# One decoder step on one core: attention with queries ahead, then eight steps of a head pair and a decode sequence; two tiles at a time where a feed-forward product begins

## The reference

```python
def mixer_mla(h, pos0, past_ckv, past_kpe, P):
    cq = rmsnorm(h @ P['mla_w_dq'], P['mla_g_q'])
    q = (cq @ P['mla_w_uq']).reshape(bsz, L, MLA_HEADS, MLA_NOPE + MLA_ROPE)      # 16 heads, 128 + 64
    q_nope, q_pe = q[..., :MLA_NOPE], rope(q[..., MLA_NOPE:], pos)
    kv = h @ P['mla_w_dkv']
    ckv = rmsnorm(kv[..., :MLA_KV_RANK], P['mla_g_kv'])                           # 256 wide
    kpe = rope(kv[:, :, None, MLA_KV_RANK:], pos)[:, :, 0]
    q_lat = jnp.einsum('blhd,rhd->blhr', q_nope, P['mla_w_uk'])
    o_lat = mla_attention(q_lat, q_pe, ckv, kpe, past_ckv, past_kpe)
    o = jnp.einsum('blhr,rhv->blhv', o_lat, P['mla_w_uv']).reshape(bsz, L, MLA_HEADS * MLA_V)
    return o @ P['mla_w_o'], ckv, kpe
```

## Time and profile before

| what | value |
|---|---|
| median of 3 runs | 3286.43 us (3283.92 to 3287.48) |
| the profiled execution, device time | 3291.61 us |
| its span, first to last instruction | 3289.7 us |
| granted TensorE clock, mean | 0.929 of full |
| TensorE busy | 90% of the span |
| VectorE / ScalarE busy | 42% / 40% |
| DMA, mean over the span | 105 GB/s |
| attention, head pairs | from 2216.7 to 2582.6 us |
| attention, decode sequences | from 2582.6 to 2743.5 us |

### The profile page before, as it was taken

The page is one execution under the profiler, slowest core; times in us unless marked ns, Lnnn a source line. Parts: engine busy times, 40 slices in busy tenths (PEclk is TensorE's granted clock), DMA queues, the critical chain, the costliest instruction groups (busy, mean ns, idle before and its releaser), DMA issues.

```text
span 3289.7 us, 56116 instructions
## 1 busy us (share of the span) xinstructions
PE 2976.2 (90%) x22503; PEld 2489.5 (76%) x22503; DVE 1379.9 (42%) x2522; ACT 1322.8 (40%) x1774; POOL 75.1 (2%) x139
## 2 busy tenths in 40 slices
PE   5999978999899989899998999989899678989996
PEld 3998858888688767799877998765665356779996
DVE  2444247788454553544335443312232213254433
ACT  3554345445222244554335553322222103365543
POOL 0000000000000000000000000000000120000000
PEclk7999988999889889999999999998999767999998
DMA  6223531222112223223432234411100474412221
GB/s 222 90 91 123 188 115 65 78 69 74 67 68 72 87 111 141 77 95 121 165 118 77 92 123 165 150 66 39 36 21 19 160 261 184 162 67 100 91 104 61
DMA packets 52952, 346.67 MB, mean 105 GB/s; under 512 B 7346, under 2 KB 7683, under 8 KB 23171
## 3 DMA queue, kind: packets, MB, share of 16 engines
q1 hardware_dynamic: 41906, 299.78, 25.4%
q0 software_dynamic: 10960, 45.71, 3.9%
HBM read 333.01 MB, written 12.45 MB: 105 GB/s over the span
## 4 chain that ended last, share of the span: by engine, by line
PE 81%; DVE 8%; ACT 4%; DVEq 2%; issue 2%; DMA 1%; ACTq 0%; SPq 0%; POOL 0%; PEldq 0%
PE PS L778 50%; PE PS L747 9%; PE PS L792 2%; PE PS L936 2%; PE PS L1132 2%; PE PS L1133 2%; PE PS L1145 1%; PE PS L1112 1%; PE PS L1187 1%; PE PS L1120 1%; PE PS L901 1%; PE PS L1162 1%; PE PS L761 1%; PE PS L800 1%; DMA weight_ring<-in_ada_w 1%
## 5 line engine op out<-in xcount | busy, mean ns | idle before, releaser
L1605 DVE TENSOR_TENSOR w_rest<-weight_ring,w_hi 128x1024 bf16<-128x1024 f32 (+1 forms) x304 | 363.7, 1197 | 960.5 <-ACT w_hi L1291 960.3
L1290 ACT ACTIVATE w_bf<-weight_ring 128x1024 bf16<-128x1024 f32 (+1 forms) x304 | 314.7, 1035 | 866.5 <-PE PS L778 859.3
L778 PE MATMUL PS<-hid_hi,w_hi 128*128 128x260 f32 x2752 | 371.6, 287 | 0.0
L778 PEld LDWEIGHTS PS<-hid_hi,w_hi 128*128 128x128 f32 x2752 | 340.1, 188 | 2.5
L778 PE MATMUL PS<-hid_rest,w_bf 128*128 128x260 bf16 x2752 | 337.6, 274 | 0.0
L778 PE MATMUL PS<-hid_bf,w_rest 128*128 128x260 bf16 x2752 | 335.6, 274 | 0.0
L1291 ACT ACTIVATE w_hi<-weight_ring 128x1024 fp32r<-128x1024 f32 (+1 forms) x304 | 309.9, 1019 | 0.0
L778 PEld LDWEIGHTS PS<-hid_bf,w_rest 128*128 128x128 bf16 x2752 | 266.6, 97 | 41.3
L778 PEld LDWEIGHTS PS<-hid_rest,w_bf 128*128 128x128 bf16 x2752 | 253.1, 97 | 44.3
L747 PE MATMUL PS<-hidden,weight_ring 128*128 128x260 f32 x896 | 206.3, 393 | 12.9 <-ACTq L504 8.9
L747 PEld LDWEIGHTS PS<-hidden,weight_ring 128*128 128x128 f32 x896 | 175.5, 197 | 42.3 <-ACTq L504 9.3
(11 more groups left out here) (386 smaller groups left out, 4168.6 us busy)
## 6 DMA issues: line engine op xcount, KB each, us to landing
weight_ring<-in_ffn_gu SPq DMA_DIRECT2D x88, 1024.0 KB, 4.8
ada_chunks<-in_ada_w SPq DMA_DIRECT2D x40, 1536.0 KB, 6.4
weight_ring<-in_ffn_wd SPq DMA_DIRECT2D x32, 1408.0 KB, 5.9
weight_ring<-in_w_hgrn SPq DMA_DIRECT2D x16, 1024.0 KB, 4.8
weight_ring<-in_ada_w SPq DMA_DIRECT2D x8, 1536.0 KB, 7.1
weight_ring<-in_w_ssm SPq DMA_DIRECT2D x8, 1536.0 KB, 6.4
weight_ring<-in_mla_pairs SPq DMA_DIRECT2D x8, 1536.0 KB, 6.4
arena<-in_pages SPq DMA_DIRECT2D x36, 288.0 KB, 5.9
```

What stands on the lines that cost most here:

```text
L778: last = pe.matmul(PS[:, bank + hf, 0:HT], w[:, buf, k * P:(k + 1) * P], x[:, first + k, hf * HT:(hf + 1) * HT], start=start and w is w_hi ...
L1290: act.activation(bf[:, buf, 0:n], src, ACT.Copy)
L1605: tt(WL_[:, buf, 0:n], W[:, slot, j * DC * P:j * DC * P + n], WH[:, buf, 0:n].bitcast(F32), ALU.subtract).then_inc(w_rest_ready, 1)
```

## The change

1. `head_pair` is split. A loop `queries` goes over all eight pairs first: query products, rotation, decode queries. The queries stay in SBUF (the 128-wide parts in `OC`, the rotary parts in `QPE`, which is `H`). Rotation's input is copied second of three.
2. The weights of a pair are loaded again for the second part, only the 8 tiles for keys and values (512 KB), under load numbers `LOADS["heads"]`.
3. Eight steps follow, written out one after the other on TensorE. Step n holds both heads of pair n and decode sequence n, interleaved by hand; the keys and values of pair n+1 are made in four pieces in between, through one PSUM bank (4). Score blocks go from the largest to the smallest, all 128-wide parts first. A head's probabilities and their transposes share one buffer for both heads.
4. In a decode sequence the exponentials use each partition's own maximum; the maximum over all partitions only gives a factor (`DST[:, 9:10]`) later on.
5. Pages lie in other buffers (parts of `Y`, `W`, the modulation chunks, the weight parts); SyncE issues all 16 of a sequence, GpSimd none. VectorE, not ScalarE, frees them.
6. `cut_group` makes w_hi first and w_bf second, each with its own semaphore; TensorE waits for w_bf before the second pass, and VectorE waits for it before it frees the slot.
7. `ffn_up` starts with `first_step`: for every normed chunk, one tile of both products.

The core of the diff:

```diff
@@ SyncE
-                    with sp.Fori(0, NB // 2) as b:
-                        for bb in range(2):
-                            sp.wait_ge(k_free[bb], b + 1)
-                            for pg in range(0, NPAGE, 2):
...
+                    base = LOADS["heads"]
+                    sp.wait_ge(w_free, base + 2)
+                    def head_weights(i, jj):
+                        slot = (base + jj) % 2
+                        sp.wait_ge(w_free, i * 2 + (base + jj + 1))
+                        sp.dma_start(WF[:, slot * HEAD_W:(slot + 1) * HEAD_W],
+                                     A["mla_pairs"][i * 2 + jj][:, 12 * P:20 * P]).then_inc(w_arrived[slot], 16)
+                    def pages_of(i, jj):
+                        sp.wait_ge(k_free[jj], i + 1)
+                        for pg in range(NPAGE):
...
+                    head_weights(0, 0)
+                    head_weights(0, 1)
+                    with sp.Fori(0, NB // 2 - 1) as i:
+                        for jj in range(2):
+                            pages_of(i, jj)
+                            head_weights(i, jj + 2)
+                    for jj in range(2):
+                        pages_of(NB // 2 - 1, jj)
+                    sp.wait_ge(k_free[0], NB // 2 + 1)
+                    sp.wait_ge(w_free, LOADS["uv"] + 2)
                     load(LOADS["uv"], 0, 0, 16, A["mla_uv"][0])
                     load(LOADS["uv"], 0, 1, 16, A["mla_uv"][1])
+                    sp.wait_ge(k_free[1], NB // 2 + 1)
@@ TensorE, start of an FFN
+                def first_step():
+                    g, buf = group(("up", s), 0, 0, 0)
+                    pe.wait_ge(gu_taken, f * FC + 1)
+                    for j in range(2):
+                        pe.wait_ge(w_bf_ready, g + j + 1)
+                        pe.wait_ge(w_rest_ready, g + j + 1)
+                    for k in range(DC):
+                        normed(k)
+                        for j in range(2):
+                            last = one_tile(2 * j, (buf + j) % 2, k, k, HH, HB, HL, k == 0, k == DC - 1)
+                            if k == DC - 1:
+                                last.then_inc(part_done, 1)
@@ TensorE, attention
+                def step(n, more):
+                    scores(n, 0)
+                    page_scores(n // 2, n % 2)
+                    transposes(n, 0)
+                    if more:
+                        key_piece(n + 1, 0)
+                    pe.wait_ge(b_m, n + 1)
+                    pe.matmul(PS[0:1, 7, 264:264 + P], DST[:, 2:3], IDENT, start=True, stop=True).then_inc(b_mt, 1)
+                    mixed(n, 0)
+                    pe.wait_ge(b_row, n + 1)
...
+                    pe.wait_ge(b_ex, n + 1)
+                    for j in range(4):
+                        pe.transpose(PS[:, 5, j * P:(j + 1) * P], PD[:, j, :], IDENT)
+                    pe.transpose(PS[0:NB, 6, 0:QR_], PDO, IDENT[0:QR_, 0:QR_]).then_inc(b_pt, 1)
+                    scores(n, 1)
+                    if more:
+                        value_piece(n + 1, 0)
+                    page_mix(n // 2, n % 2)
+                    transposes(n, 1)
+                    if more:
+                        key_piece(n + 1, 1)
+                    pe.wait_ge(b_sum, n + 1)
...
+                    mixed(n, 1)
+                    if more:
+                        value_piece(n + 1, 1)
+                    pe.wait_ge(b_on, n + 1)
...
@@ ScalarE, cut
-                act.activation(bf[:, buf, 0:n], src, ACT.Copy)
                 act.activation(hi[:, buf, 0:n], src, ACT.Copy).then_inc(w_hi_ready, 1)
+                act.activation(bf[:, buf, 0:n], src, ACT.Copy).then_inc(w_bf_ready, 1)
@@ VectorE, softmax of a head
+                def softmax(n, hh):
+                    row_max(n, hh, 3)
+                    for qb in (2, 1, 0):
+                        row_max(n, hh, qb)
+                        normalise(n, hh, qb + 1)
+                    normalise(n, hh, 0)
...
+                def step(i, jj, more):
+                    n = i * 2 + jj
+                    softmax(n, 0)
+                    own_max(n)
+                    common_max(n)
+                    softmax(n, 1)
+                    combine(n, jj)
+                    if more:
+                        queries(n + 1)
```

More of the change, by code:

```diff
@@ L1108, in head_pair, with key_piece @@
                     last.then_inc(p_ql, 1)
-                    uv = W[:, slot, 16 * P:20 * P].rearrange("p (a b) -> p a b", a=2)
-                    for c in range(NCH):
+                def key_piece(n, hh):
+                    if hh == 0:
+                        w_ready(pe, LOADS["heads"], 0, n)
+                    pe.wait_ge(p_kvc, 4 * n + 2 * hh)
+                    for k in range(RC):
+                        first = (LOADS["heads"] + n) % 2 * HEAD_W + (hh * 2 + k) * P
+                        last = pe.matmul(PS[:, 4, :], WF[:, first:first + P], CKV[:, k, 0:NP_],
+                                         start=(k == 0), stop=(k == RC - 1))
+                    last.then_inc(p_kv, 1)
@@ L1111, in head_pair, with value_piece @@
+                def value_piece(n, half):
+                    slot = (LOADS["heads"] + n) % 2
+                    uv = WF[:, slot * HEAD_W + 4 * P:(slot + 1) * HEAD_W].rearrange("p (a b) -> p a b", a=2)
+                    pe.wait_ge(p_kvc, 4 * n + 2 * half + 1)
+                    for c in (2 * half, 2 * half + 1):
                         for k in range(RC):
-                            last = pe.matmul(PS[:, 6 + c // 2, (c % 2) * 256:(c % 2 + 1) * 256],
+                            last = pe.matmul(PS[:, 4, (c % 2) * 256:(c % 2 + 1) * 256],
@@ L1199, in mla @@
                     for jj in range(2):
[L1200 removed]
+                        queries(i, jj)
                 fence()
@@ L1203, in mla @@
                     pe.sem_inc(k_free[bb], 1)
-                with pe.Fori(0, NB // 2) as b2:
-                    for bb in range(2):
-                        decode(b2, bb)
+                for half in range(2):
+                    key_piece(0, half)
+                    value_piece(0, half)
+                for n in range(NB):
+                    step(n, n + 1 < NB)
                 fence()
@@ L1519, in mla @@
+                for half in range(2):
+                    key_piece(0, 0, half)
+                    value_piece(0, 0, half)
+                with act.Fori(0, MH // 4 - 1) as i:
+                    for jj in range(2):
+                        step(i, jj, True)
+                for jj in range(2):
+                    step(MH // 4 - 1, jj, jj == 0)
                 fence()
@@ new lines, in step @@
+                def step(i, jj, more):
+                    n = i * 2 + jj
+                    softmax(n, 0)
[3 more added lines that the diff above has]
+                    combine(n, jj)
+                    if more:
+                        queries(n + 1)
+                queries(0)
+                with dve.Fori(0, MH // 4 - 1) as i:
+                    for jj in range(2):
+                        step(i, jj, True)
+                for jj in range(2):
+                    step(MH // 4 - 1, jj, jj == 0)
```

412 lines of the change are left out of this document (218 added, 194 removed).

## The result

The changed kernel takes 3146.4 us (median of 4 runs, 3144.9 to 3149.2) where the kernel before takes 3285.2 (3276.0 to 3287.5) beside it: a ratio of 0.958, with a 95% interval of 0.956 to 0.960, or 139 us less. Forecast were 3179 and a gain of 107.

A forecast was written before the change was run, and what follows sets the result against it. TensorE, busy 90% of the span, was taken as the bound, with time to gain in attention's waits and low clock. Gains of 85 + 3 + 13 + 2 + 4 = 107 us gave 3179 us from 3286.4, range 3145 to 3225.

The forecast's parts named there:

- the step: Attention, one head pair with one decode sequence: 40 us each, bounds 37.5 and 45, eight steps.
- the rival with the clock up: Attention and HGRN2: steps of 37.5 us, `mla_w_uv` at full clock, HGRN2 at its best; 3152 us, chance 0.17.
- `mla_w_uv`: Products right after attention: may run at full clock behind a dense step, 0 to 6 us less, taken as 3.
- a sign of being wrong: Inside a step: TensorE waiting for VectorE more than 3 us in total, or pages landing after their step's scores.
- the sign of being right: Chain of waits in attention: steps of 38 to 43 us, with a clock above 0.9.
- Queries and gap: Start of attention: queries of all pairs take 102 us, to 2319; first page scores at 2348, after a wait for pages.
- Waits for the softmax: Inside a step: TensorE waits 0 to 1.7 us at head 0 and 0 to 0.6 at head 1.
- the rival with lower clock: Steps: two pauses each leave half clock for 6 to 7 us, steps of 45 us; 3219 us, chance 0.17.
- FFN starts: Two tiles per normed chunk: 3.3 us less at each of four starts, 13 us in all, bounds 4 and 20.
- w_hi first: Weight copies: 2 us less at HGRN2's start and the output projections, 4 us less over eight HGRN2 heads.
- Pages and SyncE: Page loading by SyncE alone: issues 1.1 to 1.3 us apart, 22 us of slack per step hides added waits.
- The slower case: Steps: pauses and narrow page products keep the mean clock at 0.6, steps of 62 us; 3355 us, chance 0.04.

The follow-up runs named there:

- the kernel with decode apart: Changed kernel with eight steps of pairs alone, then eight of decode sequences alone, same instructions otherwise: 3303.1 us, 1.005 of the kernel before.
- both kernels with scores in separate order: Kernel before with a head's 128-wide scores ahead of its 64-wide ones: 3285.4 us; the same with weight transposes as fp32 products with the identity: 3299.1 us.
- plain products: Kernel before with the transposes of attention weights as fp32 matmuls with the identity: 3330.8 us, 1.014.
- The variant with complete blocks: Changed kernel with each score block's 128-wide and 64-wide parts one after the other, largest block first: 3137.5 us, and 3136.3 us in a second measurement.
- the two single edits: Changed kernel with one tile per normed chunk at FFN starts: 3163.0 us; changed kernel with w_bf written before w_hi: 3158.6 us.
- a second issuer: Changed kernel with odd pages issued by GpSimd: 3146.8 us, 0.957 of the kernel before.

## Why the prediction came out as it did

The sign, the order of the parts and the main mechanism (a sequence's work under a pair's) were right; the kernel with decode apart shows that the gain hangs on it. The size was not: the gain in attention was put 42 us too low (127 for 85), nearly all of that in one term, the step. The rest was 18 us for 22. The sum over the two profiled executions is 145 us; the medians are 139 apart.

That 3146 still lies in the range is luck. The range reached down to 3145 to take in the rival with the clock up, 3152; that rival wanted steps of 37.5 us, `mla_w_uv` at full clock and HGRN2 at its best. The steps are 34.0 to 36.0, all below that bound, and `mla_w_uv` did not come. What the prediction named as a sign of being wrong also came true: TensorE waits for VectorE inside a step by more than 3 us, 26.0 over eight steps and 3.2 or more in seven of them. And steps of 38 to 43 us, the sign of being right, did not come. The step was shorter than any bound because its work was overpriced, not because its waits were understood.

**Queries and gap: right.** From 2201.95 to the end of the eighth pair's queries, 2303.5, it is 101.6 us for 102; one pair takes 12.58. The first page scores started 128.2 us after the first query product, forecast 131.3, with a wait of 1.7 us for a page. The gap's parts were partly others than named: TensorE waits first for the weights of pair 0, which the prediction gives no time,

```profile
PE PS L1167 <- DMA weight_ring<-in_mla_pairs: 5.8, 1, 5.8
```

and for the pages much less than the 9 us that lie between 2319 + 20 and 2348.

**The step: 40 forecast, 34.65 measured** (277.2 us for eight). At full clock the terms were put at 35.6 us of work and 2.8 of waits, and 1.6 for clock; the fourth step has 30.87, 3.17 and none. (The waits that the prediction names, 1.7 and 0.6, make 2.3; for the other 0.5 in its 38.4 it gives no source.)
- *Scores, 11.8, are 9.3* (2.25 + 2.36 + 2.35 + 2.36). I took the duration from a kernel that goes back and forth between 128 and 64 rows and carried it over to one that does not, although the diff shows the new order. The kernel before in the new order shows 9.5.
- *Transposes, 4.1, are 2.6* (2 x 1.31). The 4.09 of the earlier trace rows is mostly a duration at half clock: its own stretch, shown above, has 0.58, and that of the fourth pair 0.52. I used the one row to argue that the clock falls there, and the other as a duration at full clock.
- *The decode part, 8.3, is 7.4* (30.87 less 9.3, 2.6 and the 11.5 of the next point). Scaling 12.0 us by a mean clock of 0.69 was a rough conversion.
- *Keys, values and products with the values* held: 3.4, 3.5 and 4.6 (2 x 1.72, 2 x 1.73, 2.36 + 2.27) for 3.45, 3.56 and 4.4.
- *Waits for the softmax* were forecast at 1.7 + 0.6 at most and are 2.3 + 0.9. The softmax was well timed: weights ready 9.9 us after the scores began (2429.66 to 2439.58), forecast 10.5. But with shorter scores there is less in front of it, so what they gain is waited for, as in the kernel before with the new order. The argument against the rival with lower clock, that these pauses are shorter than a pair's 2.0, was wrong with it: the first is 2.1 to 2.6 in steps two to eight.
- *Clock*: 1.6 us per step forecast, 0 in five steps, 1.5 and 1.9 in two; the last step is at 0.86.

**The clock at the pauses.** The earlier trace rows showed a fall at the pause before the transposes, and from it the prediction took a step of up to 45. The traces order the cases like this, each counted where the clock was at 1.00 before the pause. Behind a pause of 4.4 us (both kernels with scores in separate order) it fell in all sixteen pairs. Behind 2.0 us with twenty transposes (the kernel before) it fell in seven of seven. Behind 2.1 to 2.75 us with ten transposes and then ordinary products (the changed kernel) it fell in three of eight: in the second and third step and at the last head, while steps four to seven, with a first pause of 2.1 to 2.3, held 1.00. Behind 2.0 us with plain products it fell in one of four. So the transposes do bear on it, and that a step has ten behind a pause where a pair had twenty is a likely reason for its better clock; but pauses of one length and ten transposes went both ways, and what decides between them no run isolates.
The Trainium skill, TensorE: Matmul & The Clock Gate, Part 4: PE-mode transpose, says that a transpose does not count as TensorE activity in the way that a matmul does. The trace agrees in direction (seven of seven with transposes, one of four with plain products), but the step of 45 did not follow. TensorE's busy share alone does not tell the cases apart: a step of the changed kernel has 91%, as a pair before had the earlier trace rows, and keeps its clock more often. The variant with complete blocks, at 99%, keeps it in all seven periods.

**`mla_w_uv`: did not come.** Forecast 3 us less; both products run at clock 0.50 (7.01 and 6.98 us, for 6.27 and 6.98). The clock had fallen before, at the last wait for the softmax, 2.75 us (ten transposes in 2.41 us from 2591.91, for 1.31), and did not come back in 14 us of products of 8 columns. This part of the rival with the clock up failed although its steps came true.

**FFN starts: 3.3 forecast, 3.8 read in the trace, 3.3 to 4.2 by the edit alone.** TensorE's wait for w_hi is 0.5 us as forecast (2.1 over four starts). Full clock came earlier than assumed: 4.4 us after the first product (71.44, at 0.50 up to 75 and at 1.00 from 76), not 5.5.

**w_hi first: 6 forecast, 9 to 12 by the edit alone.** HGRN2 is 3.8 us shorter than before (forecast 4). What the term left out is the FFN starts, where w_hi of the second step is on the chain too; 0.9 of the 3.8 there belongs here, so the two single edits, 13 to 17 and 9 to 12, count it twice. Outside attention four starts and HGRN2 would make 4 x 3.8 + 3.8 = 19 us; the spans show 18.1, with the first normed chunk 1.7 us later in this execution (70.59 for 68.88).

**Pages and SyncE: right.** One late page wait of 1.7 us, issues 1.1 to 1.2 us apart (forecast 1.1 to 1.3), and a second issuer that changes nothing.

**The slower case** did not occur. The kernel with decode apart shows another way there: the same work, one head at a time and not interleaved, is 0.5% slower than before.

## What to carry to other kernels

Interleave a chain of short dependent steps with dense work where that work waits itself: a pair step took 34 to 36 us with or without a sequence in it, so the sequences became free. Before shortening an engine's work, look at what it waits for next; 2.3 us less of scores became 2.4 us more of waiting in the kernel before and 3.0 in the changed one (26.0 for 2.3 us over eight steps), and finishing the first block sooner was worth more than finishing all of them cheaply. And take durations for a sum from rows whose granted clock you have read beside them, in the order of instructions that the new kernel will have.

## What the hardware did that I had not expected

- Changing between 128 and 64 rows costs TensorE about 0.2 us a change: a head's scores take 4.7 us in two blocks of eight records (one change) and 5.9 when they alternate (seven).
- The clock can stay at 0.50 for 16 us in which TensorE has no pause (the alternating scores above), and at 1.00 across pauses of 2.1 to 2.3 us, as in four of eight steps.
- Behind the same pause of 2.02 us, twenty fp32 transposes lost the clock in seven of seven pairs, and the same transposes as plain fp32 products in one of four. They still made the kernel slower, since three pairs then lost the clock in their scores.
- SyncE starts a page every 1.18 us. Hidden for as long as a sequence has 34 us, it was the bound of the decode part when that stood alone: 19.9 us per sequence, 17.1 with two issuers.
